# Moving the issue of a table's block loads from SyncE to ScalarE

## The reference

```python
q = (hf @ w_q).reshape(N, PEER_HEADS, 2, PEER_HALF)
s1 = einsum('nhd,hkd->nhk', q[:, :, 0], sub_k1)      # 128 keys per head, top 16 of each half
s2 = einsum('nhd,hkd->nhk', q[:, :, 1], sub_k2)
...                                                  # the best 16 of 16x16 sums -> idx, gate
a = einsum('nhkd,nd->nhk', u_tab[idx], h)            # 128 rows of u_tab for each token
coef = gate * gelu(a)
out = einsum('nhk,nhkd->nd', coef, v_tab[idx])       # 128 rows of v_tab for each token
```

## Time and profile before

| | |
|---|---|
| median of 3 runs | 4558.77 us (4558.13 to 4562.73) |
| the profiled execution's own time | 4560.95 us |
| its span, first to last instruction | 4559.2 us |
| table stage, first to last product | 2840.4 to 3795.6 us |
| mean granted TensorE clock | 0.942 |

### The profile page before, as it was taken

How to read it: one execution, slowest core, us unless ns; L and a number is a source line. 1 busy time by engine, 2 the same in 40 slices (tenths; PEclk the granted TensorE clock), 3 DMA queues, 4 the chain that set the end, 5 groups by cost and what they waited for, 6 DMA issues and landing times.

```text
span 4559.2 us, 60824 instructions
## 1 busy us (share of the span) xinstructions
PE 4049.4 (89%) x23368; PEld 3503.4 (77%) x23368; DVE 3104.3 (68%) x4561; ACT 924.5 (20%) x1339; POOL 1295.2 (28%) x822
## 2 busy tenths in 40 slices
PE   7999999999899989999798989999999997676565
PEld 7999999999789987888687878887787775343221
DVE  7444344444647567888687885888898656788766
ACT  4334434323433421011001000000000004000100
POOL 0000000000000013435442432444444321667664
PEclk9999999999899999999899999999999998787777
DMA  6555677775365569999999999999999996999998
GB/s 219 198 207 191 212 287 288 282 261 188 108 238 204 200 234 422 413 403 414 415 406 373 404 423 408 405 423 424 423 413 423 424 403 280 413 390 401 422 422 353
DMA packets 303267, 1529.03 MB, mean 335 GB/s; under 512 B 36394, under 2 KB 108538, under 8 KB 134948
## 3 DMA queue, kind: packets, MB, share of 16 engines
q0 software_dynamic: 114288, 830.54, 44.0%
q1 hardware_dynamic: 188772, 695.78, 40.3%
HBM read 1450.06 MB, written 76.13 MB: 335 GB/s over the span
## 4 chain that ended last, share of the span: by engine, by line
PE 55%; DMA 27%; DVE 8%; issue 4%; DVEq 3%; ACT 2%; POOL 2%; ACTq 0%; SPq 0%; POOLq 0%
PE psum L588 27%; PE psum L654 11%; DMA sb_raw_u<-in_wstream 10%; PE psum L3343 9%; DMA sb_ring<-in_peer_v,sb_idx_all 8%; DMA sb_raw<-in_wstream 6%; PE psum L3604 2%; DVE sb_acc_b L3500 2%; POOL sb_ring L3153 2%; PE psum L2342 2%; DVEq L2371 1%; DVE sb_split L572 1%; DVE sb_acc L3179 1%; DVE sb_ring L3174 1%; ACT sb_split L568 1%
## 5 line engine op out<-in xcount | busy, mean ns | idle before, releaser
L588 PE MATMUL psum<-sb_actr,sb_split 128*128 128x264 f32 x7344 | 912.3, 286 | 28.1 <-DVE sb_split L572 14.3
L588 PEld LDWEIGHTS psum<-sb_actr,sb_split 128*128 128x128 f32 x7344 | 902.1, 190 | 32.7 <-issue 19.7
L572 DVE TENSOR_TENSOR sb_split<-sb_raw,sb_split 128x2048 fp32r<-128x2048 f32 x201 | 460.5, 2291 | 625.0 <-ACT sb_split L568 624.4
L3061 POOL DMA_INDIRECT sb_ring<-in_peer_u,sb_idx_all x256 | 417.2, 1630 | 1100.3 <-PE psum L588 522.7
L3179 DVE SCALAR_TENSOR_TENSOR sb_acc<-sb_ring,sb_coef,sb_acc 128x2048 f32<-128x2048 f32 x256 | 601.8, 2351 | 162.0 <-DMA sb_ring<-in_peer_v,sb_idx_all 147.2
L3174 DVE CUSTOM_DVE_ANT_0 sb_ring<-sb_ring,sb_htok 128x2048 f32<-128x2048 f32 x264 | 595.5, 2290 | 157.6 <-DMA sb_ring<-in_peer_u,sb_idx_all 127.6
L3061 POOL DMA_INDIRECT sb_ring<-in_peer_v,sb_idx_all x256 | 403.9, 1578 | 655.0 <-DVE sb_acc L3179 577.5
L3604 PE MATMUL psum<-sb_ring,sb_diag 128*128 128x512 f32 x512 | 353.7, 854 | 241.2 <-DMA sb_ring<-in_peer_v,sb_idx_all 234.0
L3500 DVE SCALAR_TENSOR_TENSOR sb_acc_b<-sb_ring,sb_coef_b,sb_acc_b 128x2048 f32<-128x2048 f32 x192 | 451.4, 2351 | 127.2 <-DMA sb_ring<-in_peer_v,sb_idx_all 113.9
L3153 POOL DMA_INDIRECT sb_ring<-in_peer_v,sb_idx_all x256 | 442.3, 1728 | 247.8 <-DVE sb_acc_b L3500 124.3
L3343 PE MATMUL psum<-sb_h2b,sb_raw 128*128 128x256 f32 x2048 | 457.9, 383 | 25.5 <-DMA sb_raw<-in_wstream 25.5
(11 more groups left out here) (455 smaller groups left out, 4351.0 us busy)
## 6 DMA issues: line engine op xcount, KB each, us to landing
sb_raw<-in_wstream SPq DMA_DIRECT2D x398, 1024.0 KB, 7.6
sb_raw_u<-in_wstream SPq DMA_DIRECT2D x64, 1024.0 KB, 23.0
sb_states<-in_state SPq DMA_DIRECT2D x32, 512.0 KB, 3.9
sb_states_t<-in_stateT SPq DMA_DIRECT2D x32, 512.0 KB, 4.4
out_gla_s<-sb_states SPq DMA_DIRECT2D x32, 512.0 KB, 3.0
dram_z<-sb_zst SPq DMA_DIRECT2D x121, 132.0 KB, 3.7
dram_z_b<-sb_zst SPq DMA_DIRECT2D x65, 128.0 KB, 1.8
sb_vrow<-dram_v SPq DMA_DIRECT2D x8, 1024.0 KB, 5.6
```

Source lines behind the costliest of these rows:

```text
L572: nc.vector.tensor_tensor(split[:, slot, 1, :], raw[:, slot, :], split[:, slot, 0, :], ALU.subtract).then_inc(lo_ready, 1)
L588: last = nc.tensor.matmul(psum[:, bank, 0:ntok], w[a], acts(b, kt), start=(i == 0 and a == 0 and b == 0), stop=(i == len(kts) - 1 and a == 1))
L3061: nc.gpsimd.indirect_dma_start(ring[g % RING][:], None, ins[table], bass.IndirectOffsetOnAxis(ap=col, axis=0)) \
```

## The change

The load of block k + 4 is issued by ScalarE, behind its wait for the end of block k and ahead of its two copies of that block. SyncE keeps the first four loads of the stage and all 128 stores. Buffers, semaphores and their values are the same.

```diff
-        def load_u(sp, i):
-            sp.dma_start(raw_u[u_slot(i)], ins["wstream"][N_END + i]).then_inc(raw_landed[u_slot(i)], 16)
+        def load_u(eng, i):
+            eng.dma_start(raw_u[u_slot(i)], ins["wstream"][N_END + i]).then_inc(raw_landed[u_slot(i)], 16)
...
             for k in range(NU):
-                if k + RAWS < NU:
-                    sp.wait_ge(out_ready, OUTS_U + k + 1)
-                    load_u(sp, k + RAWS)
                 sp.wait_ge(evac_done, OUTS_U + k + 1)
                 sp.dma_start(a_dram[:, k, :], a_stage[:, k % 4, :]).then_inc(z_stored[k % 4], 16)
...
         def act_table(act):
             for i in range(NU):
                 act.wait_ge(out_ready, OUTS_U + i + 1)
+                if i + RAWS < NU:
+                    load_u(act, i + RAWS)
                 if i >= 4:
                     act.wait_ge(z_stored[i % 4], 16 * z_stores_u(i))
```

## The result

The changed kernel takes 4573.04 us in the median of 20 runs (4564.93 to 4579.21), the kernel before 4558.77 (4552.5 to 4566.51, 20 runs): a ratio of 1.0030 [1.0024, 1.0036]. By the ratio it is 13.7 us slower (the medians lie 14.3 apart), 19 us above the forecast and 1 us above the range. The profiled execution took 4564.93 us, 4.0 more than the one before, and is the fastest of the 20.

The account below looks back on a forecast made before the run. The prediction took the nearly full DMA engines (403 to 424 GB/s) as the bound, with loads late from sharing turns with stores. 4560.95 - 8.1 + 2.0 + 0.3 = 4555.2, forecast as 4554 us; range 4543 to 4572.

Parts of the forecast that it names:

- Issue: 124 block loads of 0.33 us move from SyncE to ScalarE, which has waiting time to cover them: cost 0.
- Loads: Loads in their own queue land in about 9.4 us; TensorE takes 6.91 us a block, saving 70 us of its time.
- Rival 1: Nothing changes: loads take turns as before or their wait isn't the stores' doing; 4561 us, chance 0.17.
- End of stage: VectorE's 8.1 us wait for TensorE before the first pick goes; VectorE itself is 2.0 us late, plus 0.3.
- rival 2: Slower: behind TensorE's early end gather rows stay near 3.53 us, so VectorE ends late; 4575 us, chance 0.16.
- New waits: ScalarE's exp behind block 68 waits 20 us for VectorE, holding loads; the DMA shortfall costs 3.6 us; block 102 nothing.
- Rows: Gathers lose what loads gain, total bytes needed by VectorE's last row unchanged; 1.6 us regained from fuller DMA engines.

Follow-up runs that it names:

- e3: Changed kernel with ScalarE issuing the stores as well as the loads, so both share one queue again; ratio 0.9999 to the kernel before.
- e4: Kernel before with the stores of two blocks joined into one, 64 stores with packets of 1 KB; ratio 1.0015 to the kernel before.
- e1: Changed kernel with the roles swapped: SyncE issues only the loads, ScalarE the stores, queues still apart; ratio 0.9993 to the kernel before.
- e2: Changed kernel with ScalarE's two exps moved from behind blocks 68 and 102 to behind 78 and 106; ratio 1.0007 to the kernel before.
- after_again: The changed kernel measured once more, unaltered; ratio 1.0027 to the kernel before.
- e5: Changed kernel with SyncE issuing loads, ScalarE stores, and the two exps moved to behind blocks 78 and 106; ratio 0.9999 to the kernel before.

## Why the prediction was wrong

**Issue: right.** No load cost TensorE anything by ScalarE's time; in e3 ScalarE issued both kinds and the ratio was 0.9999.

**Loads: right.** The third queue, 6.91 us a block, 58 us of TensorE's time; e3 and e4 confirm that sharing turns with the stores was the cause. Two waits are left, one of them the 13.35 us, where I had 0 to 5. Rival 1 is out. The sentence of the Trainium skill that it cites (DMA: Bandwidth & Descriptors, Issuing engines are not separate DMA queues), that several issuers save only the sequencer's time, holds here for the total, 423 GB/s as before, but not for a single load, which landed in 9.1 and 9.5 us in e1 and in 9.2 and 9.9 in e2 instead of 23.0. The trace of after gives no landings for its loads.

**End of stage: right in the gap, wrong in what ends it.** The 8.1 us went (0.20 us remain). But VectorE's share ended past 3800, at 3807.8, which I had named as the sign of being wrong. Rows behind TensorE's end came at 2.49 us, so rival 2's place is refuted; its sign came true by another mechanism.

**New waits: the step that failed, by its size.** The wait was named at its place, behind block 68, and I priced it at 12 x 0.3 = 3.6 us. Measured, the stretch lost 12.7 us more than before, and e2, which takes the wait away, gives back 15.5 - 4.8 = 10.7. Both factors were too small.
- The length. I scaled VectorE's arrival evenly (3337) and got a wait of 20 us with load 73 out at 3339. It was 29.5 us and 3347.4. The two searches took the same 29.1 us as before, so the 10 us were lost ahead of them. From 2992 to the first search the gathers' queue moved 84.17 MB in 325.75 us, 258 GB/s where I had 262, and VectorE still had 78 row tiles to do, one more than before at that time. By an estimate the slower rows are 7 us of it and the one row 4.
- The depth. I took 30% from the hole at 3320 of before, whose row gives (423 - 318)/423 = 25%. That hole had loads in it. Without loads, a search of 10 us leaves the DMA engines with nothing once the ring is full: 154 GB/s over 24 us, (423 - 154)/423 = 64% below full, and 24 x 0.64 = 15.3 us.

**Rows: wrong, smaller.** Here a term stood at nothing without a reason. I let TensorE end 70 us earlier and took all from the first pick on as before, but SyncE's first loads of the next stage wait for TensorE alone. They came ahead of VectorE's last row: 2.3 MB more on the direct queues, 5.4 us, and 0.7 MB less on the gathers' queue, 3.8 us together. The 1.6 us to be regained didn't come either. Instead 2.6 and 2.8 us leaked in the stretches ahead of and behind the hole, where nothing had leaked before. For the second stretch part has a name: the exp behind block 102 waits for VectorE too (47.6 - 29.5 = 18.1 us), and from 3565 to 3580 the rate is 386 where it was 423. The first leak is 2.2 to 2.4 us in after, after_again and e2 and at most 0.5 where SyncE issued the loads in a queue of their own; its cause isn't shown.

In sum, from the stage's start to the first pick: forecast -8.1 + 3.6 - 1.6 + 0.3 = -5.8 us, measured +11.4. Of the 17.2 between, 9.1 are the hole (12.7 - 3.6), 3.8 the bytes, and 4.3 the rest: the leaks, 5.4, and the 1.6 that stayed, less 2.3 in the stage's first 70 us (6.7 instead of 9.0, no more than traces of the same program differ) and 0.5 behind 3640. The forecast of 4554 was also 1 us above its own sum, 4555.2 - 2.2 = 4553.0.

## What to carry to other kernels

- When a DMA issue moves to another engine, list every wait that now stands ahead of it in that engine's order, and ask of each what else fills the DMA engines while it lasts. If it waits for the engine that also frees the buffers of the other traffic, both streams stop together; price the hole at the full rate then, not at the rate of a hole in which one stream still ran.
- Speeding up an engine that isn't the bound makes the engines next to it arrive early at waits that never showed. Here TensorE's 58 us gave nothing, opened a wait of 29 us and put 2.3 MB of later transfers ahead of the engine that was the bound.
- Under saturated DMA engines, count bytes and empty time, not waits: taking 45 us of waiting for loads away brought the first pick 2.2 us forward in e1 and 3.0 in e5, and one hole put it back by 12.7.

## What the runs showed of the hardware

- A second issuing engine is a queue with turns of its own. How long a load takes under full DMA engines follows the stores that it shares a queue with, by number and not by bytes: 23.0 us with one store of 128 packets of 512 B per load, 10.4 with the same bytes in half as many packets of 1 KB (e4), 9.4 with none. Whether a turn is one packet, as the prediction reads it, or a whole DMA, no run tells: loads, stores and gathers all have 128 packets.
- Stores left the busy queue for an almost empty one and landed in 9.0 us (e1) against 25.1, though the engines were as full.
- TensorE's granted clock fell in its stop of 13.35 us, to 0.50 (1.2 GHz) from 3347 to 3356. It was 0.78 in the mean of 3355 to 3362, and the first block behind the stop took 8.60 us against 7.07 of the one ahead of it; the next two took 13.98, as ever. So the stop cost TensorE 1.5 us beyond its length, which nobody waited for.
